# Attention over the memory one head at a time, opening tiles chunk by chunk, and four row gathers issued at four places

## The chip, the cores and the metric

The kernel runs on one core of one Trainium2 chip. The metric is the device time of one execution in microseconds; the time of a kernel is the median of its runs. A profile comes from one execution of its own, whose time may differ a little from that median.

The engines are called as in the profile: PE is TensorE (PEld its weight loads), DVE is VectorE, ACT is ScalarE, POOL is GpSimd, SP is SyncE. Each works through its own queue in order and waits on semaphores.

## The reference

A decoder trunk of two layers on 256 tokens with 1024 channels. Each layer has a token mixer (gated convolution and forgetting attention), a cross-attention over 256 memory tokens, and a SwiGLU channel mixer: dense in layer 0, top 2 of 8 experts in layer 1. The parts that matter here:

```python
def mem_cross_attention(h, m, w_q, w_kv, g_q, g_k):
    q = rmsnorm((h @ w_q).reshape(B, S, XA_HEADS, XA_HEAD_DIM), g_q)      # 4 heads x 128
    kv = (m @ w_kv).reshape(B, M, 2, XA_HEADS, XA_HEAD_DIM)
    k = rmsnorm(kv[:, :, 0], g_k)
    v = kv[:, :, 1]
    s = jnp.einsum('bshd,bmhd->bhsm', q, k) * (XA_HEAD_DIM ** -0.5)
    p = jax.nn.softmax(s, axis=-1)
    return jnp.einsum('bhsm,bmhd->bshd', p, v).reshape(B, S, XA_WIDTH)

for l in range(DEPTH):
    x = x + mixer(rmsnorm(x, g_mix[l])) @ w_out[l]
    x = x + mem_cross_attention(rmsnorm(x, g_xa[l]), rmsnorm(mem, g_mem[l]), ...) @ w_xo[l]
    x = x + (swiglu or moe_swiglu)(rmsnorm(x, g_ffn[l]), ...)
# moe: top-2 of 8 experts per token, softmax of the two logits as weights, sum of the two experts' outputs
```

## The kernel before

**Products.** Every large product is made of three: inputs and weights are split into a high part (ACT, a copy that rounds to fp32r) and a low part (DVE, the value less the high part), and PE adds high x high, low x high and high x low. Weights come in *fills*: SP loads each into one of four slots of `ring`, ACT writes its high part to `wh`, DVE its low part to `wl` (two buffers each, three for the high parts in the expert passes). A slot of `ring` is free when DVE has made the low part; `wh` when PE's high products are done (`highs_used`), `wl` when the low products are. In the queues of ACT and DVE these splits stand at places written out by hand (`high_of`, L765, and `low_of`, L1112).

**PSUM.** Eight banks. `layer_results` lists the results in order, each with the bank it takes (a pair names the result whose bank it inherits, a single name takes the next of `plan.order`). PE waits in `open_bank` until the bank's former result has been read.

**Opening tile.** `channel_tile` (from L1648) makes 128 output channels for 256 tokens from 8 input chunks. Its first call on a new input (`inputs` given) comes while ACT is still writing the chunks' high parts (`input_high`, L795, or L984 for the gate product) and DVE their low parts (`input_low`, L1132): eight products high x high, each pair of chunks behind a wait, then eight with the weights' low part, then eight with the inputs' low part. It is called so for the query projection of each layer (`yT`) and for the first gate tile of layer 0 (`zT`). Each product is 256 wide and shows as L1616.

**Attention over the memory.** The query projection has four tiles, one for each head, two to a bank (`xq0`, `xq1`) and two to a fill. DVE multiplies a pair of heads by the gain (`query_gained`, L1327); ACT squares the pair (L962); PE sums the squares (`query_means`, products with `selh`), DVE adds epsilon (`query_mean`, L1332), and POOL raises to the power -1/2 (L699). PE makes the scores of a head (`memory_scores`, `xk`), DVE their maximum (`memory_max`, L1341, then L1344 with POOL's result), ACT the exponentials (`memory_exps`, L940, two for a head), DVE the normalisation (`probs_normalised`, L1349 and L1350), PE the transposes (`memory_probs`, L1972), DVE or ACT the copy (`probs_copied`, L1354, L949), and PE the sum over the memory (`memory_heads`, `xv`, one bank for two heads), split by ACT (L954) and DVE (L1131). The output projection `xw` runs by slots of two heads each: sixteen high products 512 wide (L1612, L1613), then the second pair of heads (`memory_heads(1)`, put inside), then eight products with the low weights. PE's order is tiles 0 to 2, means of the first pair, tile 3, scores 0 and 1, means of the second pair, scores 2 and 3, transposes 0 and 1, heads 0 and 1, transposes 2 and 3, projection.

**Expert passes.** Layer 1 runs the eight experts one after another, each in a pass of 24 fills: 16 of gate and up weights, 8 of down weights. A token's normalised row stands in the DRAM table `rows_of`, 128 rows to an expert. In every pass POOL stores the results of the expert before to that table (L723) and, after the up product of the first half, loads the next expert's rows (L720); in the last pass no rows are left to load. Instead POOL gathers each token's finished result rows from the table (L734): two choices for each of two token tiles, 128 rows of 4 KB each, four transfers in all. It issues all four as soon as the store of pass seven is done and the last rows have been transposed. DVE adds them to the residual behind the low parts of slots 20 to 23 (`rows_added`, L1519). Slots are counted from 0 here.

```python
            for t in range(TT):
                for c in range(2):
                    nc.gpsimd.indirect_dma_start(rows_got[t][c], None, rows_of, bass.IndirectOffsetOnAxis(ap=rows[:, t, c:c + 1], axis=0)
                                                 ).then_inc(rows_back[2 * t + c], 16)
```

## Time and profile before

| | us |
|---|---|
| median of 3 runs | 1349.35 |
| lowest and highest | 1347.03, 1351.03 |
| the profiled execution's own time | 1347.77 |
| its span, first to last instruction | 1346.2 |
| PE, DVE, ACT, POOL busy | 1316.9, 1019.1, 831.3, 92.0 |
| mean granted TensorE clock | 0.995 |

A span is the time from the first to the last instruction of the profiled execution. Matmuls are pipelined and overlap in the rows: the distance of two starts is what one costs, and the duration is longer. A product of plain fp32 operands shows as two records. The memory attention of layer 0 lies near 155 to 185 us, that of layer 1 near 525 to 555 us; the passes over the experts fill the time from 574 us on, the last from 1241.6 us.

### The profile page before, as it was taken

Reading aid. Unit: us, or ns where it says so; the run is one execution under the profiler, and the core shown is the slowest. Engines: PE = TensorE matmul, PEld = TensorE weight load, DVE = VectorE, ACT = ScalarE, POOL = GpSimd, SP = SyncE. Lnnn points to the kernel's source line nnn. Section 1 sums busy time; section 2 is a strip of 40 time slices with the busy share of each in tenths; the row PEclk is TensorE's granted clock in tenths of the full one; section 3 lists DMA queues with packets and bytes.
Section 4 is the critical chain, followed back from the end, with each engine's and each line's share of the span. In section 5 each row is a group of like instructions: output and inputs, shape, how many; then the busy total and the mean of one; then the engine's idle time right before and its main releaser. Section 6 shows DMA issues by size and latency. Waiting matters only on the chain.

```text
span 1346.2 us, 18754 instructions
## 1 busy us (share of the span) xinstructions
PE 1316.9 (98%) x7213; PEld 1146.7 (85%) x7213; DVE 1019.1 (76%) x782; ACT 831.3 (62%) x738; POOL 92.0 (7%) x98
## 2 busy tenths in 40 slices
PE   7999999999999999899999999999999999999998
PEld 6998879999889988788888888888888888888786
DVE  4758665545366586588888888888889888888888
ACT  5545454343355454477777777678677677777674
POOL 4201010000012010010000000000000000000300
PEclk9999999999999999999999999999999999999999
DMA  8633535554498334289999899899999998998994
GB/s 305 201 119 122 171 136 188 194 182 143 155 316 327 118 122 164 81 326 393 337 414 384 338 409 387 343 412 371 356 388 355 394 380 342 417 385 336 414 386 164
DMA packets 120910, 386.24 MB, mean 287 GB/s; under 512 B 6064, under 2 KB 47644, under 8 KB 120860
## 3 DMA queue, kind: packets, MB, share of 16 engines
q1 hardware_dynamic: 108972, 365.09, 71.8%
q0 software_dynamic: 3168, 11.54, 2.2%
q10 hardware_dynamic: 8720, 8.91, 1.9%
q8 instruction: 36, 0.59, 0.2%
q14 instruction: 14, 0.11, 0.0%
HBM read 369.79 MB, written 15.73 MB: 286 GB/s over the span
## 4 chain that ended last, share of the span: by engine, by line
PE 85%; DVE 7%; ACT 4%; issue 2%; DMA 1%; POOL 1%; SPq 0%; DVEq 0%; ACTq 0%
PE bank L1616 40%; PE bank L1612 21%; PE bank L1613 21%; DVE wl L1112 3%; PE bank L2112 1%; ACT wh L765 1%; DMA ring<-in_we_up 1%; DVE wl L1126 1%; ACT scratch L940 1%; DVE scratch L1259 1%; ACT wh L779 1%; DVE scratch L1237 1%; ACT aT L795 1%; DVE aT_low L1131 1%; PE bank L1792 0%
## 5 line engine op out<-in xcount | busy, mean ns | idle before, releaser
L1126 DVE TENSOR_TENSOR wl<-ring,wh 128x2816 fp32r<-128x2816 f32 (+1 forms) x127 | 400.3, 3171 | 54.6 <-PE bank L1616 42.7
L779 ACT ACTIVATE wh<-ring 128x2816 fp32r<-128x2816 f32 (+1 forms) x128 | 336.6, 2631 | 141.7 <-PE bank L1613 49.1
L1112 DVE TENSOR_TENSOR wl<-ring,wh 128x2048 fp32r<-128x2048 f32 (+2 forms) x69 | 186.6, 2704 | 94.1 <-ACT wh L765 84.3
L1126 DVE TENSOR_TENSOR wl<-ring,wh_third 128x2816 fp32r<-128x2816 f32 (+1 forms) x64 | 187.0, 2923 | 32.4 <-PE bank L1616 28.1
L1612 PE MATMUL bank<-wh,xh 128*128 128x512 f32 x528 | 198.7, 376 | 4.1 <-DVE wl L1126 2.8
L765 ACT ACTIVATE wh<-ring 128x2048 fp32r<-128x2048 f32 (+1 forms) x68 | 152.6, 2244 | 78.8 <-PE bank L1616 38.1
L1613 PE MATMUL bank<-wh,xl 128*128 128x512 f32 x528 | 197.7, 374 | 0.0
L1616 PE MATMUL bank<-wl,xh 128*128 128x512 f32 (+1 forms) x768 | 194.9, 375 | 0.0
L779 ACT ACTIVATE wh_third<-ring 128x2816 fp32r<-128x2816 f32 (+1 forms) x64 | 155.5, 2429 | 35.1 <-DMA ring<-in_we_up 14.8
L1616 PEld LDWEIGHTS bank<-wl,xh 128*128 128x128 f32 x768 | 141.7, 188 | 18.5
L1612 PE MATMUL bank<-wh,ah 128*128 128x512 f32 x328 | 128.7, 393 | 1.7 <-DVE wl L1112 1.7
L1613 PE MATMUL bank<-wh,al 128*128 128x512 f32 x328 | 127.9, 390 | 0.0
L1612 PEld LDWEIGHTS bank<-wh,xh 128*128 128x128 f32 x528 | 99.1, 188 | 23.4 <-issue 4.9
L1613 PEld LDWEIGHTS bank<-wh,xl 128*128 128x128 f32 x528 | 99.2, 188 | 15.2
L1616 PE MATMUL bank<-wl,ah 128*128 128x512 f32 x440 | 112.0, 389 | 0.0
L1612 PE MATMUL bank<-wh,aT 128*128 128x512 f32 (+2 forms) x272 | 98.5, 371 | 0.8 <-DVE scratch L1237 0.5
L1616 PEld LDWEIGHTS bank<-wl,ah 128*128 128x128 f32 x440 | 82.6, 188 | 17.1
L1613 PE MATMUL bank<-wh,aT_low 128*128 128x512 f32 (+2 forms) x272 | 96.9, 365 | 0.0
L1612 PE MATMUL bank<-wh_third,xh 128*128 128x512 f32 (+1 forms) x240 | 90.6, 377 | 0.0
L1613 PE MATMUL bank<-wh_third,xl 128*128 128x512 f32 (+1 forms) x240 | 90.2, 376 | 0.0
L1616 PE MATMUL bank<-xh,wh 128*128 128x256 f32 x352 | 86.4, 284 | 0.8 <-ACT xh L984 0.8
L1616 PE MATMUL bank<-xl,wh 128*128 128x256 f32 x352 | 85.5, 283 | 0.0
(262 smaller groups left out, 1924.4 us busy)
## 6 DMA issues: line engine op xcount, KB each, us to landing
ring<-in_we_gate SPq DMA_DIRECT2D x64, 1408.0 KB, 7.6
ring<-in_we_up SPq DMA_DIRECT2D x64, 1408.0 KB, 7.7
ring<-in_we_down SPq DMA_DIRECT2D x56, 1536.0 KB, 8.4
ring<-in_w_in SPq DMA_DIRECT2D x8, 1536.0 KB, 11.7
ring<-in_w_in SPq DMA_DIRECT2D x10, 1024.0 KB, 6.8
ring<-in_w_gate SPq DMA_DIRECT2D x6, 1536.0 KB, 6.7
ring<-in_w_up SPq DMA_DIRECT2D x6, 1536.0 KB, 6.6
ring<-in_w_down SPq DMA_DIRECT2D x6, 1536.0 KB, 6.6
```

The source lines that it names most:

```text
L765: nc.scalar.activation(wh[:, j, 0:n], ring[:, slot, 0:n], ACT.Copy).then_inc(high_ready, 1)
L779: nc.scalar.activation(wh_in_pass(j, n), ring[:, slot, 0:n], ACT.Copy).then_inc(high_ready, 1)
L795: ins = nc.scalar.activation(aT[:, c, :], bank(l, f"{names}{i}")[:, k * S:k * S + S], ACT.Copy, scale=col(l, gain, c))
L940: ins = nc.scalar.activation(xsc[:, h, q, :], bank(l, f"xs{h}")[:, q * S:q * S + S], ACT.Exp, bias=xnm[:, h, q:q + 1], scale=xqr[:, h, q:q ...
L1112: nc.vector.tensor_tensor(wl[:, j, 0:n], ring[:, slot, 0:n], wh[:, j, 0:n].bitcast(F32), ALU.subtract).then_inc(low_ready, 1)
L1126: nc.vector.tensor_tensor(wl[:, j % 2, 0:n], ring[:, j % NSLOT, 0:n], wh_in_pass(j, n).bitcast(F32), ALU.subtract).then_inc(low_ready, 1)
L1131: return nc.vector.tensor_tensor(dst, src, high_.bitcast(F32), ALU.subtract)
L1237: nc.vector.scalar_tensor_tensor(sc[:, h, :], bank(l, f"s{h}")[:, 0:3 * P], HD ** -0.5, mask[:], ALU.mult, ALU.add).then_inc(take(l, f"s{h ...
L1259: then_wait(nc.vector.scalar_tensor_tensor(acc[:, back:S], u[:, 0:S - back], col(l, "tap", 8 - 4 * back + j), acc[:, back:S], ALU.mult, AL ...
L1612: nc.tensor.matmul(dst, x_high, w_high, start=first, stop=False)
L1613: return nc.tensor.matmul(dst, x_low, w_high, start=False, stop=False)
L1616: return nc.tensor.matmul(dst, lhsT, rhs, start=first, stop=last)
```

## The change

Three things are changed.

1. **Opening tile.** In `channel_tile` with `inputs`, each high x high product is followed at once by the product with the weights' low part of the same chunk. The wait for the low part stands ahead of the tile. The eight products with the inputs' low part come last, as before. The query projection's first tile now has its own bank and signals its end.
2. **Memory attention.** Each head has a bank of its own for its query tile, and gain, square, means, epsilon and power are done for one head at a time: the means go to two spare columns of the head's own bank. The orders of PE, ACT, DVE and POOL are rewritten so that heads follow each other: a tile of the projection, the means and scores of the head before it, the transposes of the head before that. The last head's transposes stand inside the output projection, ahead of the second pair of heads. Banks of later results follow from a new list, `AFTER_MEMORY`, and the scratch region into which ACT writes squares that nobody reads moves from 5120 to 1024.
3. **Gathers.** POOL issues the first gather where it was. Ahead of the second it waits for the up product of the first half to be done (`uA2`, after slot 7), ahead of the third for the transposed hidden block `hA2` (after slot 10), ahead of the fourth for the up product of the second half (`uB2`, after slot 15). Each wait is followed by a one-element addition.

The core of the diff:

```diff
-    names += [f"yT{i}" for i in range(4)] + ["xq0", "xq1"]
-    names += ["xqm0", "xs0", "xs1", "xqm1", "xs2", "xs3", "xpt0", "xpt1", "xo0", "xpt2", "xpt3"]
-    names += [f"xw{i}" for i in range(4)] + ["xo1"] + [f"zT{i}" for i in range(4)]
+    names += ["yT0", "yT1", ("yT2", "wo0"), ("yT3", "wo1"), ("xq0", "wo2"), ("xq1", "wo3"), ("xq2", "oT0"), ("xq3", "oT1")]
+    names += [(f"xqm{h}", f"xq{h}") for h in range(4)] + [(f"xs{h}", f"yT{h}") for h in range(4)]
+    names += [(f"xpt{h}", f"xqm{h}") for h in range(4)] + [("xo0", "xs0")]
+    names += [("xw0", "xpt0"), ("xw1", "xpt1"), ("xw2", "xs1"), ("xw3", "xs2"), ("xo1", "xo0")]
+    names += [("zT0", "xs3"), ("zT1", "xpt2"), ("zT2", "xpt3"), ("zT3", "xo1")]
...
             for t in range(TT):
                 for c in range(2):
+                    if t + c > 0:
+                        pool.wait_ge(*lfull(("uA2", "hA2", "uB2")[2 * t + c - 1], rounds * NE - 1))
+                        then_wait(nc.gpsimd.tensor_tensor(zeros[0:1, 1:2], zeros[0:1, 2:3], zeros[0:1, 3:4], ALU.add))
                     nc.gpsimd.indirect_dma_start(rows_got[t][c], None, rows_of, bass.IndirectOffsetOnAxis(ap=rows[:, t, c:c + 1], axis=0)
                                                  ).then_inc(rows_back[2 * t + c], 16)
...
+                query_square(0)
+                high_of(l, "xo", 0)
+                query_square(1)
+                memory_exps(0)
+                query_square(2)
+                memory_exps(1)
+                query_square(3)
+                probs_copied(1)
+                memory_exps(2)
+                heads_high(0)
+                memory_exps(3)
                 high_of(l, "xo", 1)
-                probs_copied(1)
-                memory_exps(2, 3)
-                heads_high(0)
                 probs_copied(3)
                 heads_high(1)
...
                 if inputs is not None:
                     pe.wait_ge(high_ready, n + 1)
+                    pe.wait_ge(low_ready, n + 1)
                     for k in range(KT):
                         if k % 2 == 0:
                             pe.wait_ge(acthigh_ready, HIGHS[fill[0], inputs] + k // 2 + 1)
                         mm(ps, w_high[:, k, :], x_high[:, k, :], k == 0, False)
-                    pe.wait_ge(low_ready, n + 1)
-                    for k in range(KT):
                         mm(ps, w_low[:, k, :], x_high[:, k, :], False, False)
...
+                query_tile(0)
+                query_tile(1)
+                query_means(0)
                 for i in range(2):
                     pe.wait_ge(*taken(l, f"mkT{i}"))
-                memory_scores(0, 1)
+                memory_scores(0)
+                query_tile(2)
                 query_means(1)
-                memory_scores(2, 3)
-                memory_probs(0, 1)
+                memory_scores(1)
+                memory_probs(0)
+                query_tile(3)
+                query_means(2)
+                memory_scores(2)
+                memory_probs(1)
+                query_means(3)
                 for t in range(TT):
                     pe.wait_ge(*taken(l, f"mv{t}"))
                 memory_heads(0)
-                memory_probs(2, 3)
-                token_projection("xw", "xo", XH, range(2), {j: taken(l, f"xo{j}") for j in range(2)}, lambda: memory_heads(1))
+                memory_scores(3)
+                memory_probs(2)
+
+                def last_heads():
+                    memory_probs(3)
+                    memory_heads(1)
+
+                token_projection("xw", "xo", XH, range(2), {j: taken(l, f"xo{j}") for j in range(2)}, last_heads)
```

DVE's order in the memory attention, from the first gain to the first normalisation. TENSOR_SCALAR to `scratch` is a gain, SCALAR_TENSOR_TENSOR a mean's epsilon, TENSOR_REDUCE a maximum, RECIPROCAL with the TENSOR_TENSOR behind it a normalisation, TENSOR_TENSOR to `wl` the low part of a fill. Before:

```order
L1323 TENSOR_SCALAR msq<-msq 128x2
L1112 TENSOR_TENSOR wl<-ring,wh 128x2048
L1327 TENSOR_SCALAR scratch<-bank,vcols 128x512
L1112 TENSOR_TENSOR wl<-ring,wh 128x2048
L1332 SCALAR_TENSOR_TENSOR xqr<-bank,msq 128x4
L1336 ISA
L1327 TENSOR_SCALAR scratch<-bank,vcols 128x512
L1341 TENSOR_REDUCE xnm<-bank 128x2
L1344 TENSOR_TENSOR xnm<-xnm,xqr 128x2
L1341 TENSOR_REDUCE xnm<-bank 128x2
L1344 TENSOR_TENSOR xnm<-xnm,xqr 128x2
L1349 RECIPROCAL xden<-xden 128x2
```

After the change:

```order
L1336 TENSOR_SCALAR scratch<-bank,vcols 128x256
L1371 TENSOR_SCALAR msq<-msq 128x2
L1124 TENSOR_TENSOR wl<-ring,wh 128x2048
L1336 TENSOR_SCALAR scratch<-bank,vcols 128x256
L1340 SCALAR_TENSOR_TENSOR xqr<-bank,msq 128x2
L1343 ISA
L1348 TENSOR_REDUCE xnm<-bank 128x2
L1351 TENSOR_TENSOR xnm<-xnm,xqr 128x2
L1124 TENSOR_TENSOR wl<-ring,wh 128x2048
L1336 TENSOR_SCALAR scratch<-bank,vcols 128x256
L1356 RECIPROCAL xden<-xden 128x2
```

A gain is for one head now, the first maximum stands ahead of the second fill's low part, and the first normalisation follows that low part and a further gain.

PE's order from the means of the second head to those of the third. The tile products have `aT`, means `selh`, scores `xk`, and transposes `ident`. After the change:

```order
L1632 MATMUL bank<-aT,wl 128x256 x8
L1632 MATMUL bank<-selh,scratch 128x1 x2
L1632 MATMUL bank<-xk,scratch 128x256 x2
L1988 MATMUL bank<-ident,scratch 128x128 x4
L1632 MATMUL bank<-aT,wh 128x256
L1632 MATMUL bank<-aT_low,wh 128x256
```

Before, the same kinds of work, from the last products of the last query tile:

```order
L1616 MATMUL bank<-aT,wl 128x256 x8
L1616 MATMUL bank<-xk,scratch 128x256 x4
L1616 MATMUL bank<-selh,scratch 128x1 x4
L1616 MATMUL bank<-xk,scratch 128x256 x4
L1972 MATMUL bank<-ident,scratch 128x128 x8
L1616 MATMUL bank<-scratch,xv 128x256 x4
```

The first head's transposes now stand ahead of the fourth query tile; before, all tiles and all scores came first.

POOL's order at the end of the program, the gathers and what stands between them, after the change:

```order
L735 TENSOR_TENSOR zeros<-zeros 1x1
L741 DMA memT<-rows_of,rows 128x1024
L739 REGISTER_ALU
L740 TENSOR_TENSOR zeros<-zeros 1x1
L741 DMA row_spare<-rows_of,rows 128x1024
L739 ISA
L740 TENSOR_TENSOR zeros<-zeros 1x1
L741 DMA xk<-rows_of,rows 128x1024
L739 REGISTER_ALU
L740 TENSOR_TENSOR zeros<-zeros 1x1
L741 DMA xv<-rows_of,rows 128x1024
```

Before, the four stood one behind another, behind the first addition. Now each of the last three has a wait and an addition ahead of it.

## Rows read from the trace of the kernel before

**Rows 1.** The page's first part: engine, busy us (share of the span), instructions.
```profile
PE 1316.9 (98%) x7213; PEld 1146.7 (85%) x7213; DVE 1019.1 (76%) x782; ACT 831.3 (62%) x738; POOL 92.0 (7%) x98
```

**Rows 2.** Windows: us, busy (records) per engine, PEclk, DMA share, GB/s; passes seven, eight.
```profile
1147.00:1241.60 94.60, 94.60 (x452) 80.78 (x451) 82.01 (x45) 69.99 (x47) 2.67 (x3) 1.00 0.96 377
1147.00:1181.40 34.40, 34.40 (x164) 29.63 (x163) 30.68 (x13) 26.49 (x15) 2.67 (x3) 1.00 1.02 416
1241.60:1276.00 34.40, 31.60 (x148) 26.71 (x147) 28.78 (x18) 21.96 (x13) 12.71 (x7) 1.00 1.01 413
```

**Rows 3.** Waits of PE, layer 1, 521 to 575 us: total, times, longest.
```profile
PE bank L1972 <- DVE scratch L1350: 1.8, 3, 1.0
```

**Rows 4.** Timeline, layer 1's opening tile: start, us, engine, line, op, tiles, count, idle before.
```profile
522.26 3.03 ACT L795 ACTIVATE aT<-bank,vcols 128x256 fp32r<-128x256 f32 x8 [1.61 <-PE bank L1635]
523.20 3.23 DVE L1132 SCALAR_TENSOR_TENSOR aT_low<-bank,vcols,aT 128x256 fp32r<-128x256 f32 x8 [1.34 <-ACT aT L795]
...
525.68 1.12 PE L1616 MATMUL bank<-aT,wl 128*128 128x256 f32 x8
...
526.64 1.12 PE L1616 MATMUL bank<-aT_low,wh 128*128 128x256 f32 x8
```

**Rows 5.** Timeline, the opening tile of layer 0's gate product, PE.
```profile
195.53 1.11 PE L1616 MATMUL bank<-xh,wl 128*128 128x256 f32 x8
```

**Rows 6.** Timeline, the same stretch, PE: means, transposes, last heads, low products.
```profile
538.85 1.02 PE L1616 MATMUL bank<-selh,scratch 128*128 128x1 f32 x8
...
539.74 1.97 PE L1616 MATMUL bank<-xk,scratch 128*128 128x256 f32 x8
...
547.13 0.63 PE L1972 MATMUL bank<-ident,scratch 128*128 128x128 f32 x4 [0.47 <-DVE scratch L1350]
...
551.41 1.89 PE L1616 MATMUL bank<-scratch,xv 128*128 128x256 f32 x8
552.94 2.18 PE L1616 MATMUL bank<-wl,aT 128*128 128x512 f32 x8
554.96 0.39 PE L1612 MATMUL bank<-wh,aT 128*128 128x512 f32 x1
```

**Rows 7.** Timeline, layer 1's memory attention on the engines beside PE.
```profile
528.36 2.29 DVE L1112 TENSOR_TENSOR wl<-ring,wh 128x2048 fp32r<-128x2048 f32 x1
...
530.68 0.75 DVE L1327 TENSOR_SCALAR scratch<-bank,vcols 128x512 f32<-128x512 f32 x1
...
536.46 1.01 POOL L699 TENSOR_TENSOR xqr<-xqr,neghalf 128x4 f32<-128x4 f32 x1 [30.85 <-DVEq L1336]
...
538.19 0.69 DVE L1341 TENSOR_REDUCE xnm<-bank 128x2 f32<-128x512 f32 x1
...
539.12 0.56 ACT L940 ACTIVATE scratch<-bank,xnm,xqr 128x256 f32<-128x256 f32 x1 [0.34 <-DVE xnm L1344]
...
540.55 0.69 DVE L1350 TENSOR_TENSOR scratch<-scratch,xden 128x512 f32<-128x512 f32 x1
```

**Rows 8.** Timeline of POOL, last pass: the first and the last of four gathers.
```profile
1249.91 1.06 POOL L734 DMA_INDIRECT memT<-rows_of,rows  x1 [0.28 <-POOL zeros L731]
...
1258.31 3.86 POOL L734 DMA_INDIRECT xv<-rows_of,rows  x1 [0.30 <-issue]
```

**Rows 9.** Chain of waits: the same low products of passes seven and eight.
```profile
1180.25 1.29 PE bank L1616 x6
...
1278.13 1.28 PE bank L1616 x6
```

**Rows 10.** Timelines: slot 6 in pass seven (ACT), in pass eight (ACT, PE).
```profile
1162.72 2.56 ACT L779 ACTIVATE wh<-ring 128x2816 fp32r<-128x2816 f32 x1 [0.89 <-DMA ring<-in_we_gate]
...
1261.11 2.56 ACT L779 ACTIVATE wh<-ring 128x2816 fp32r<-128x2816 f32 x1 [3.51 <-DMA ring<-in_we_gate]
...
1267.03 0.47 PE L1612 MATMUL bank<-wh,xh 128*128 128x512 f32 x1 [2.37 <-DVE wl L1126]
```

**Rows 11.** Timeline of DVE, last pass: the low part of slot 6.
```profile
1263.79 3.09 DVE L1126 TENSOR_TENSOR wl<-ring,wh 128x2816 fp32r<-128x2816 f32 x1 [1.57 <-ACT wh L779]
```

More of the change, by code:

```diff
@@ L135, in build @@
                 plan.add((l, n))
+        plan.order, plan.turn = [plan.at[l, m][0] for m in AFTER_MEMORY], 0
         if l == 0:
@@ L955, in heads_high, with query_square @@
                                          bank(l, f"xo{i}")[:], ACT.Copy).then_inc(yhigh_ready, 1)
[L957 to L964 removed]
+                def query_square(h):
+                    act.wait_ge(*full(l, f"xq{h}"))
+                    act.wait_ge(xq_gained, XH * l + h + 1)
+                    nc.scalar.activation(sq[:, 4 + h, :], bank(l, f"xq{h}")[:, 0:S], ACT.Square).then_inc(take(l, f"xq{h}"), 1)
+                query_square(0)
[9 more added lines that the diff above has]
+                memory_exps(3)
                 high_of(l, "xo", 1)
[L966 to L968 removed]
                 probs_copied(3)
```

96 lines of the change are left out of this document (45 added, 51 removed).

## The prediction

> **What bounds the kernel now.** The page comes first: PE holds records for 98% of the span [rows 1], so only what shortens PE's work or its gaps can move the end. The windows show where gaps are. A middle pass over an expert has PE busy for 94.60 of 94.60 us at a granted clock of 1.00, with DMA at 0.96; in its first 34.4 us DMA is at 1.02, full. The last pass has 31.60 busy us in the same 34.4, so 2.8 us of gap [rows 2]. The other gaps lie in the attention over the memory, once per layer: 1.8 us in three waits of the transposes for DVE's normalised probabilities [rows 3]. Ahead of it the opening tile of the query projection is paced: ACT writes the eight input chunks in 3.03 us, DVE their low parts in 3.23 us, and PE does the eight products with the weights' low parts only when the last chunk is there [rows 4]. Three places, then: openings, attention, gathers.
>
> **Openings.** The eight low-weight products start at 525.68 and the next eight at 526.64: 0.12 us each [rows 4]. Six of them now run while ACT makes the chunks (one pair of chunks per about 0.75 us, four products take 0.48). The last pair of highs is there at 525.3, so PE is through with them at 525.8; six products with the low inputs follow to 526.5, and the last low chunk is there at 523.20 + 3.23 = 526.43, just in time. The tile ends 0.7 earlier. The new wait for the weights' low part ahead of the tile costs nothing: DVE made it before the residual. The same helper opens layer 0's gate product, where the pattern is the same [rows 5]: 0.7 too. What is late next there is PE itself.
>
> **Memory attention, per layer.** PE's work stays: 0.96 us for eight tile products, 0.9 for a pair of means (538.85, then 539.74), about 0.8 for a head's scores, 0.55 for a head's transposes, 1.53 for a pair of heads (551.41 to 552.94), 0.23 for each product 512 wide [rows 6]. What moves is who waits. I lay the new order out on layer 1's clock with these durations: DVE's weight low part 2.29, a gain 128x512 0.75 (taken as 0.42 for half), a max 0.69, a normalisation 0.69 and 0.2 of reciprocal, an exponential 0.56 twice for a head, a power on POOL 1.01 (for half the elements 0.75 to 1.01) [rows 7], 0.05 to 0.3 for each hop.
> PE: tile 0 ends 526.8, tile 1 529.7, means 0 and scores 0 530.9, tile 2 533.8, means 1 and scores 1 535.0. DVE: its weight low part keeps it until 530.65 [rows 7], then gain 1, mean 0, max 0 (behind POOL's power) to 532.5, the next weight low part to 534.85, gain 2, normalisation 0 at 536.2. So PE waits 1.2 us ahead of transposes 0. Then tile 3 to 539.7, means 2, scores 2 540.9; DVE, held by the wait for tile 3, ends normalisation 1 at 541.15: 0.3 of wait. Transposes 1, means 3, heads 0 to 543.7, scores 3 to 544.5; normalisation 2 ends 544.65: 0.2. The projection's sixteen high products start at 545.4 behind DVE's low part of the heads and hide head 3's maximum, exponentials and normalisation (ready 548.3). Head 3's transposes and the second pair of heads end at 551.3, the eight low products at 553.1; ACT's and DVE's copies of the second pair take as long, so the next slot starts near 553.2. Before, it started at 554.96 [rows 6]: 1.8 saved, opening included. A check from the other side: 29.7 us passed since the last chunk, and PE's work in them is 26.6 (90 tile products 10.8, means 1.7, scores 3.3, transposes 2.2, heads 3.1, 24 wide products 5.5), so 3.1 was waiting; now 27.9 with 25.9 of work leave 2.0.
> In layer 0 everything stands as in layer 1, 370 us earlier; behind it ACT and DVE split the first gate slot in the order of their queues, ahead of the residual sum. Both start from the second pair of heads, so this too comes 1.8 earlier. Added instructions: per layer two gains, two means, two squares, two powers; they are in the layout. The bank changes and the moved scratch region cost nothing, since each bank taken has been read 5 us or more before.
> Weighed against a rule: by the row, a gain of 128x512 takes 0.75, and a chunk of 128x256 in the same form 3.23/8 = 0.40 [rows 4, 7], so halving adds 0.05 per pair, and the sum stays. The Trainium skill (VectorE: DVE Perf Modes, "The TRN2 errata") says that each small operation pays a fixed latency and advises at least 512 elements; with its 150 cycles (0.16 us, an estimate from that page) four extra DVE operations per layer would cost 0.6 each layer if all were on the path, and the sum would be 5.3 instead of 6.5.
>
> **Gathers.** Four transfers of 0.52 MB start between 1249.91 and 1258.31 [rows 8], 5.1 us of DMA at 413 GB/s, in the stretch where DMA is full [rows 2]. By the chain the same products come at 1180.25 and 1278.13; a pass is 94.60, so the last pass loses 3.3 us [rows 2, 9]. Slot 6 (the seventh of 24) is converted 19.5 us after the pass began, in the pass before 15.7 [rows 2, 10]. The change leaves the first gather there (1.27 us), puts the second where every other pass loads 0.52 MB of rows, and the others after a hidden block and after the last up product. Of 5.1 us of extra transfer 1.8 were swallowed, so 1.27 alone would be. But DVE has one-off work in this pass (the last pass's weights), which also makes it late: slot 6's low part would, without the wait of 1.57 for ACT, start near 1262.4 and end 1265.5 [rows 11]; PE is free at 1267.03 - 2.37 = 1264.66 [rows 10], and starts that slot only with the low part. So about 1 us of loss stays and 2.2 go. Bounds: 1.3 (two gathers' worth still felt) and 3.3 (nothing lost). The later gathers are cheap if the later slots' slack holds; they are first needed by DVE after slots 21 to 23, 15 us or more after issue, and POOL has nothing behind its new waits.
>
> **Sum.** 2 x 1.8 + 0.7 + 2.2 = 6.5 us off the profiled execution's 1347.77: 1341.3. The median of the three runs is 1.58 above that execution, so 1342.8. A measurement tells about 0.3%, 4 us: faster means under 1345.3.
>
> **Rivals.** (a) The gathers' load only moves. The bytes are the same, DMA is at 0.96 in a whole pass [rows 2], so a late gather can starve a down slot as an early one starved slot 6; against it, the last pass fetches nothing for a next one. Gain 0 there: 4.3 saved, 1345.0. The Trainium skill (DMA: Bandwidth & Descriptors, "Issuing engines are not separate DMA queues") says that transfers of every issuing engine run on the same 16 DMA engines and interleave; the trace agrees so far that slot 6 was late beside POOL's gathers.
> (b) The round trip scores, maximum, power, exponentials, normalisation is longer than the tile, means and scores that cover it. It is 535.0 to 536.2 late already at head 0. If each of three heads waits 0.8 more, 4.8 goes back: 1347.6, no change.
> (c) The same mechanism on the other side: DVE is in order, and gain 3 and the weight low part stand ahead of a normalisation that PE waits for. At 1.1 us more at each of six rounds the saving is gone, above 1.8 it is slower; with 2.3, as long as one weight low part [rows 7], it is 13.8 - 6.5 = 7.3 slower: 1356.6. For it: one chain of four heads on one DVE, busy for most of that time. Against: the page of before shows two rounds with waits of at most 1.0 [rows 3].
> (d) All waits vanish: 1.9 more per layer and 1.1 in the pass, 11.4 saved, 1337.9.
>
> **How the numbers follow.** Forecast 0.60, own range 1340.5 to 1344.5; (a) 0.15; (b) 0.12; (c) 0.06; (d) 0.07. Of (a), at the edge of what can be told, 0.10 counts as faster and 0.05 as same. Faster 0.60 + 0.07 + 0.10 = 0.77, same 0.12 + 0.05 = 0.17, slower 0.06. The range takes in (a), half of (d) and the run-to-run spread of 2 us: 1339.5 to 1346.5.
>
> **What would show it.** In the profile after: in layer 1 the opening tile's low-input products end about 0.7 earlier against the last chunk; three waits of transposes near 1.2, 0.3 and 0.2; the second projection slot 27.9 us after the last input chunk (now 29.7). In the last pass slot 6 starts with a wait near 1, not 2.37, four gathers stand apart, and PE has no new gap after slot 8. Wrong would be waits of PE over 2 us at a head, a PE gap beside the third or fourth gather, or a granted clock below 1.00 in the attention.

## The result, and the profile after

| | before | after |
|---|---|---|
| median of 5 runs, us | 1349.68 | 1341.64 |
| lowest and highest | 1347.03, 1351.03 | 1339.31, 1342.32 |
| the profiled execution's own time | 1347.77 | 1339.31 |
| its span | 1346.2 | 1337.7 |

The ratio is 0.9942, 95% interval 0.9929 to 0.9956: faster by 8.0 us, with 5.9 to 9.6 inside the interval. The prediction said 1342.8 and a gain of 6.5. Beside the experiments below the kernel before ran 9 to 29 times each, with medians of 1347.8 to 1348.1, so the 1349.68 here lies high: against those medians the changed kernel is 6.1 to 6.5 us faster, and the stretches below give 7.5.

The page's first part after the change. PE is still at 98%, with 1.9 us less of records [rows 1]:

```profile
PE 1315.0 (98%) x7213; PEld 1145.5 (86%) x7213; DVE 1020.1 (76%) x790; ACT 831.8 (62%) x742; POOL 84.2 (6%) x105
```

**Where the time went.** In both profiles I took the starts of the same six events and subtracted. PE's transposes of the token mixer near 51 us stand for the start; then come the first input chunk of layer 1's query projection, DVE's `hT` (the router's input), ACT's table load behind the router, the first low products on the hidden block in pass seven, and the last such group of six in the last pass. The rows of after:

```profile
51.08 1.04 PE L1769 MATMUL bank<-ident,scratch 128*128 128x128 f32 x8
...
519.68 3.03 ACT L802 ACTIVATE aT<-bank,vcols 128x256 fp32r<-128x256 f32 x8 [1.62 <-PE bank L1651]
...
557.05 1.29 DVE L1149 TENSOR_TENSOR hT<-bank,vcols 128x512 f32<-128x512 f32 x2 [0.41 <-PE bank L1651]
...
557.89 3.71 PE L1632 MATMUL bank<-wr,hT 128*128 128x8 f32 x32 [0.22 <-DVE hT L1149]
...
563.99 1.28 ACT L1031 ACT_TABLE_LOAD   x1
...
1205.95 1.52 PE L1632 MATMUL bank<-wl,ah 128*128 128x512 f32 x6
...
1327.52 1.52 PE L1632 MATMUL bank<-wl,ah 128*128 128x512 f32 x6
```

Before (its first chunk is in [rows 4]):

```profile
50.78 1.04 PE L1752 MATMUL bank<-ident,scratch 128*128 128x128 f32 x8
...
561.72 1.29 DVE L1137 TENSOR_TENSOR hT<-bank,vcols 128x512 f32<-128x512 f32 x2 [0.40 <-PE bank L1635]
...
563.11 4.61 PE L1616 MATMUL bank<-wr,hT 128*128 128x8 f32 x32 [0.77 <-DVE hT L1137]
...
570.11 1.28 ACT L1019 ACT_TABLE_LOAD   x1
...
1212.16 1.53 PE L1616 MATMUL bank<-wl,ah 128*128 128x512 f32 x6
...
1336.03 1.52 PE L1616 MATMUL bank<-wl,ah 128*128 128x512 f32 x6
```

| stretch | before | after | gain | forecast |
|---|---|---|---|---|
| start to layer 1's first chunk (all of layer 0) | 471.48 | 468.60 | 2.88 | 1.8 + 0.7 |
| first chunk to `hT` (layer 1's attention) | 39.46 | 37.37 | 2.09 | 1.8 |
| `hT` to table load (router) | 8.39 | 6.94 | 1.45 | 0 |
| table load to pass seven | 642.05 | 641.96 | 0.09 | 0 |
| pass seven to the end of the last pass | 123.87 | 121.57 | 2.30 | 2.2 |

They sum to 8.81, less 0.30 of a later start: the 8.5 us between the spans. The router's 1.45 us was in no term of mine.

**Layer 1's attention.** Of PE's waits between 518 and 575 us in after, those up to the router's first product:

```profile
PE bank L1988 <- DVE scratch L1357: 0.5, 2, 0.4
PE bank L1632 <- ACT aT L802: 0.4, 1, 0.4
PE bank L1632 <- DVE hT L1149: 0.2, 1, 0.2
```

The transposes now wait 0.5 us in all, 1.8 before [rows 3]. The timeline of the same stretch:

```profile
523.35 1.12 PE L1632 MATMUL bank<-aT_low,wh 128*128 128x256 f32 x8
...
524.50 0.48 DVE L1336 TENSOR_SCALAR scratch<-bank,vcols 128x256 f32<-128x256 f32 x1 [0.65 <-PE bank L1632]
...
528.67 0.70 POOL L703 TENSOR_TENSOR xqr<-xqr,neghalf 128x2 f32<-128x2 f32 x1 [25.69 <-DVEq L1343]
...
532.37 0.69 DVE L1357 TENSOR_TENSOR scratch<-scratch,xden 128x512 f32<-128x512 f32 x1
...
533.21 0.63 PE L1988 MATMUL bank<-ident,scratch 128*128 128x128 f32 x4 [0.37 <-DVE scratch L1357]
...
538.17 0.63 PE L1988 MATMUL bank<-ident,scratch 128*128 128x128 f32 x4 [0.15 <-DVE scratch L1357]
...
550.28 0.39 PE L1628 MATMUL bank<-wh,aT 128*128 128x512 f32 x1
```

The low-input products of the opening tile start 3.67 us after the first chunk, 4.38 before [rows 4]: 0.71 won. The second projection slot starts at 550.28, 27.57 us after the last chunk (519.68 + 3.03).

**The last pass.** Windows, as in [rows 2], of pass seven, of its first 34.4 us, and of the last pass's:

```profile
1140.72:1235.32 94.60, 94.60 (x452) 80.78 (x451) 82.01 (x45) 69.71 (x48) 1.95 (x3) 1.00 0.96 377
1138.90:1173.30 34.40, 34.40 (x163) 29.59 (x162) 30.07 (x13) 26.78 (x15) 1.95 (x3) 1.00 1.02 417
1233.50:1267.90 34.40, 33.57 (x158) 28.65 (x157) 31.19 (x21) 24.93 (x15) 5.57 (x6) 1.00 1.02 415
```

PE's gap in the last pass is 0.8 us where it was 2.8. Slot 6 on ACT, DVE and PE, then the gathers on POOL:

```profile
1253.15 2.56 ACT L786 ACTIVATE wh<-ring 128x2816 fp32r<-128x2816 f32 x1 [1.70 <-DMA ring<-in_we_gate]
...
1256.02 3.09 DVE L1138 TENSOR_TENSOR wl<-ring,wh 128x2816 fp32r<-128x2816 f32 x1 [0.21 <-DVE ffn L1518]
...
1259.26 0.47 PE L1628 MATMUL bank<-wh,xh 128*128 128x512 f32 x1 [0.83 <-DVE wl L1138]
```

```profile
1243.78 3.91 POOL L741 DMA_INDIRECT memT<-rows_of,rows  x1 [0.36 <-POOL zeros L735]
...
1267.63 0.97 POOL L741 DMA_INDIRECT row_spare<-rows_of,rows  x1 [0.27 <-POOL zeros L740]
...
1280.33 0.96 POOL L741 DMA_INDIRECT xk<-rows_of,rows  x1 [0.27 <-POOL zeros L740]
...
1299.49 0.96 POOL L741 DMA_INDIRECT xv<-rows_of,rows  x1 [0.27 <-POOL zeros L740]
```

ACT's wait for the gate weights fell from 3.51 to 1.70 us [rows 10] in this pair of profiles, and DVE no longer waits for ACT ahead of slot 6 (1.57 before [rows 11]). It comes straight from a one-off operation of the last pass (L1518).

### The profile page after: what moved, and what is told of

The parts are those of the page before. It is cut to its first block, busy times and chain, and to the rows that moved or that the text cites. A ratio compares the mean times of both kernels' runs of the same rounds, so it can differ in the third digit from the quotient of the medians.

```text
span 1337.7 us, 18771 instructions
## 1 busy us (share of the span) xinstructions
PE 1315.0 (98%) x7213; PEld 1145.5 (86%) x7213; DVE 1020.1 (76%) x790; ACT 831.8 (62%) x742; POOL 84.2 (6%) x105
## 4 chain that ended last, share of the span: by engine, by line
PE 87%; DVE 8%; ACT 2%; issue 1%; DMA 1%; POOL 1%; SPq 0%; DVEq 0%; ACTq 0%
PE bank L1632 40%; PE bank L1628 22%; PE bank L1629 22%; DVE wl L1124 3%; PE bank L2140 1%; DVE wl L1138 1%; ACT wh L772 1%; DMA ring<-in_we_gate 1%; DVE scratch L1271 1%; DVE scratch L1249 1%; DVE aT_low L1143 1%; PE bank L1809 0%; POOL mfox L672 0%; ACT wh L786 0%; PE bank L1651 0%
## 5 line engine op out<-in xcount | busy, mean ns | idle before, releaser
L1124 DVE TENSOR_TENSOR wl<-ring,wh 128x2048 fp32r<-128x2048 f32 (+2 forms) x69 | 186.6, 2705 | 94.5 <-ACT wh L772 84.6
L1632 PEld LDWEIGHTS bank<-wl,ah 128*128 128x128 f32 x440 | 82.6, 188 | 17.1
```

Source lines behind the costliest of these rows:

```text
L1124: nc.vector.tensor_tensor(wl[:, j, 0:n], ring[:, slot, 0:n], wh[:, j, 0:n].bitcast(F32), ALU.subtract).then_inc(low_ready, 1)
L1632: return nc.tensor.matmul(dst, lhsT, rhs, start=first, stop=last)
```

## The experiments

Theory: the three parts act on their own (openings 0.7 each, head-by-head order about 1.4 per layer, gathers 2.2 to 2.7), and a fourth effect, the bank of the router's result, explains what I had missed. Twelve kernels were run; every one has a profile, so the same stretches can be compared. "Half clock" is the time between 558 and 580 us in which PEclk was 0.50 (1.2 of 2.4 GHz), added up from windows of 0.5 us. The other columns are differences of starts as above, in us.

| kernel | median | ratio to before, interval | start to chunk | chunk to `hT` | `hT` to table | `hT` to pass 7 | pass 7 to end | half clock |
|---|---|---|---|---|---|---|---|---|
| before | | | 471.48 | 39.46 | 8.39 | 650.44 | 123.87 | 10.2 |
| b_gathers_alone | 1346.32 | 0.9985 (0.9976, 0.9994) | 471.47 | 39.50 | 8.22 | 650.15 | 121.54 | 10.2 |
| b_opening_alone | 1346.66 | 0.9989 (0.9980, 0.9999) | 470.01 | 38.77 | 9.57 | 651.63 | 123.27 | 13.7 |
| b_router_bank | 1347.33 | 0.9996 (0.9987, 1.0004) | 471.52 | 39.47 | 7.32 | 649.46 | 123.64 | 10.2 |
| a_attention_alone | 1346.30 | 0.9981 (0.9970, 0.9992) | 473.10 | 39.48 | 6.94 | 649.11 | 122.64 | 6.8 |
| a_opening_undone | 1344.95 | 0.9971 (0.9960, 0.9982) | 469.94 | 38.04 | 7.06 | 651.69 | 121.67 | 10.2 |
| a_gathers_together | 1343.25 | 0.9967 (0.9956, 0.9978) | 468.59 | 37.35 | 6.94 | 648.90 | 124.24 | 6.8 |
| a_router_bank | 1343.40 | 0.9961 (0.9948, 0.9974) | 468.61 | 37.40 | 9.22 | 652.23 | 121.50 | 13.7 |
| after | 1341.64 | 0.9942 (0.9929, 0.9956) | 468.60 | 37.37 | 6.94 | 648.90 | 121.57 | 6.8 |
| c_oneoffs_later | 1343.13 | 0.9965 (0.9952, 0.9979) | 468.62 | 37.38 | 6.94 | 649.69 | 122.40 | 6.8 |
| c_first_gather_later | 1342.86 | 0.9961 (0.9948, 0.9975) | 468.65 | 37.34 | 8.43 | 652.22 | 122.66 | 13.7 |
| c_gathers_all_late | 1342.65 | 0.9961 (0.9948, 0.9975) | 470.22 | 37.38 | 7.06 | 649.45 | 122.49 | 10.2 |
| c_both_later | 1342.19 | 0.9958 (0.9944, 0.9971) | 468.67 | 37.34 | 8.19 | 650.28 | 121.65 | 10.2 |
| d_spread | 1340.93 | 0.9940 (0.9928, 0.9952) | 468.60 | 37.41 | 8.28 | 651.08 | 120.59 | 13.7 |

Where nothing was changed the first two stretches and the last repeat within 0.1 us, but for places named below; the medians scatter by more than most single edits are worth. The stretches therefore carry the argument, and the medians say only whether it holds in sum. By the ratios the three parts alone give 2.0 (gathers), 1.5 (openings) and 2.6 us (attention), 6.1 together, and the whole change 7.8; the intervals reach 1.2 to 1.9 us to either side, so the two agree, but weakly.

Two entries under `hT` to pass 7 hold a loss that belongs to no edit. Between the same products of neighbouring passes 94.6 to 94.7 us lie everywhere else, but 96.87 once in a_opening_undone and 95.75 once in c_first_gather_later. In the first ACT waited for weights in the middle of a pass that has no gathers:

```profile
872.48 2.56 ACT L786 ACTIVATE wh<-ring 128x2816 fp32r<-128x2816 f32 x1 [4.40 <-DMA ring<-in_we_gate]
```

The four weight transfers issued from 862.3 on took 10.0 to 11.4 us to land there, those in the same place of after 6.9 to 8.5. Why is open.

**Opening tiles: undone in after, and alone in before.**

The edit against after; b_opening_alone has its reverse, in the kernel before.

```diff
-                    pe.wait_ge(low_ready, n + 1)
                     for k in range(KT):
...
                         mm(ps, w_high[:, k, :], x_high[:, k, :], k == 0, False)
+                    pe.wait_ge(low_ready, n + 1)
+                    for k in range(KT):
                         mm(ps, w_low[:, k, :], x_high[:, k, :], False, False)
```

> The changed kernel with the opening tile's products in their old order (eight high, then eight with the weights' low part). My theory: each of three openings (query projection of both layers, gate product of layer 0) is 0.7 us longer and nothing hides it, 2.1 us slower than the change in all, about 1343.7. Rival (the head-by-head order hides the late tile, since DVE's chain sets the pace there): only layer 0's gate product counts, 0.7 us; the PE wait ahead of the first transposes falls from 0.4 to 0.

> The kernel before, with each high product of an opening tile followed by the low-weight product of its chunk and nothing else. My theory: three openings of 0.65 to 0.7 us each, 2.0 us in all: 0.65 in layer 0's attention, 0.65 at layer 0's gate tile, 0.65 in layer 1; time 1345.8. Rival: the tile's gain is taken back by the next wait (PE comes earlier to a product that DVE's low part of the second fill holds, or to the transposes): then the transposes' waits grow from 1.8 to 2.4 and 0.7 us or less is left of each attention.

Chunk to `hT` is 0.67 longer without the new order and 0.69 shorter with it alone. The whole of layer 0 (start to chunk), which has two openings, is 1.34 longer and 1.47 shorter. So 0.67 to 0.74 for an opening, three times, and nothing is given back. The rival of b_opening_alone, a growing wait at the transposes, fell: they wait 1.8 us there as before. So did that of a_opening_undone, a late tile hidden by DVE's chain: PE still waits ahead of the first transposes, 0.28 where after has 0.37. The median of b_opening_alone is only 1.3 us below before; the difference to 2.1 is within what its runs scatter (1343.5 to 1350.2). That of a_opening_undone is 3.3 above after, not 2.1; in its profile, besides the 2.0 of the openings, 2.3 us are the loss in a middle pass named above.

```profile
535.95 0.63 PE L1989 MATMUL bank<-ident,scratch 128*128 128x128 f32 x4 [0.28 <-DVE scratch L1357]
```

**Attention head by head alone** (after with both other parts undone).

> The changed kernel with both other parts undone: gathers all at once, old order in the opening tiles; what is left is the attention head by head (with its bank plan). The three parts add up if they are independent: the whole is 8.0 us, gathers 2.5, openings 2.0, so this one is 3.5 us faster than before: 1.2 to 1.4 in each layer's attention and 0.5 to 1.4 around the router. Time 1344.3 where before is 1347.8. Rival: the attention has most of its gain only with the new opening, because the round trips through DVE start from it; then under 2 us is left.

By the stretches of a_opening_undone, which has the same attention and old openings, the head-by-head order is worth 39.46 - 38.04 = 1.42 in layer 1, and 471.48 - 469.94 = 1.54 in layer 0. With 0.7 for the opening this gives 2.1 to 2.2 per layer. No run takes the order of the heads, their banks and the moved scratch region apart; the 1.4 to 1.5 is for all of these together. But a_attention_alone itself shows 39.48 in layer 1, nothing won, and its median is 1.6 us below before, not 3.5: taken alone, that is what the rival forecast. The windows say why:

```profile
523.50:527.50 4.00, 3.02 (x19) 2.19 (x18) 2.82 (x8) 3.77 (x9) 0.00 (x0) 1.00 0.36 149
527.50:531.00 3.50, 3.50 (x19) 3.50 (x18) 0.97 (x5) 2.12 (x4) 0.00 (x0) 0.52 0.03 5
```

The same two stretches of the program in a_opening_undone, by distance from the first chunk:

```profile
521.55:525.55 4.00, 3.02 (x19) 2.19 (x18) 2.83 (x8) 3.77 (x9) 0.00 (x0) 1.00 0.35 148
525.55:529.05 3.50, 3.50 (x32) 3.50 (x31) 2.10 (x5) 2.48 (x4) 0.00 (x0) 1.00 0.02 5
```

In one the granted clock is 0.52 and 19 products have records, in the other 1.00 and 32. The program is the same here, and so is PE's work in the 4 us ahead (3.02 us busy in both), so this is a matter of the execution, not of the order. It cost 39.48 - 38.04 = 1.44 us. The windows show two more such stretches in that profile, at 155.0 to 159.5 (0.62) and 350 to 360 (0.83); after has none between its start event at 51 us and the router. Start to chunk is 3.2 us longer than in a_opening_undone, which has the same program up to there and neither stretch. Without the three, the stretches would add up as the theory says. Its twelve runs lie between 1343.0 and 1349.1, but such stretches do not explain this: the run of 1349.14 had a mean granted clock of 0.994, one of 1347.93 had 0.996, and the three with 0.992, the profiled one among them, 1346.1 to 1347.9. What scatters the runs of one kernel is open.

**Gathers: together again in after, and at four places in before.** The edit takes out or puts in the waits for `uA2`, `hA2`, `uB2` and their additions.

> The changed kernel with its four gathers issued at one place again. My theory (the early gathers starve slot 6 of the last pass): the last pass loses 3.3 us again instead of about 1, so this is 2.3 us slower than the change, about 1344; slot 6 of the last pass starts with a wait near 2.4 us. Rival (the gathers' load only moves, and the shorter last pass came from something else): no difference to the change, 1341.6, and the wait stays near 0.8.

> The kernel before, with the gathers issued at the four places and nothing else. My theory: 2.3 to 2.7 us less in the last pass (97.9 us between the same low products of passes seven and eight becomes 95.3 to 95.6), PE's waits there 0.8 instead of 2.8; time 1345.3 on a scale where before is 1347.8. Rival: what the gathers give depends on the shorter attention ahead of them; then less than 1.5.

Pass seven to the end grows by 2.67 in one and shrinks by 2.33 in the other. The size is as expected, the place is not: a_gathers_together has no wait of 2.4 us at slot 6, but 1.17 there, 1.05 at slot 7 and 0.78 further on. Its PE waits for low parts in the last pass, and ACT's rows for slots 6 and 7:

```profile
PE bank L1625 <- DVE wl L1135: 3.0, 3, 1.2
```

```profile
1252.56 2.57 ACT L783 ACTIVATE wh<-ring 128x2816 fp32r<-128x2816 f32 x1 [1.54 <-DMA ring<-in_we_gate]
...
1258.43 2.55 ACT L783 ACTIVATE wh<-ring 128x2816 fp32r<-128x2816 f32 x1 [3.31 <-DMA ring<-in_we_up]
```

So the 3.51 of slot 6 in before [rows 10] is one way in which the same delay falls. In the other four profiles with four gathers at the start slot 6 waits 1.2 to 1.5 us and slots 7 and 8 2.8 to 3.3 each. The sum of ACT's waits ahead of slots 6, 7 and 8 is steady: 7.4 to 7.8 us with four gathers (five profiles), 4.0 with one (five; in a_opening_undone one of the three waits is put down to PE), 2.7 with none (four).

That the gathers' worth depends on what stands ahead is not seen: 2.33 and 2.67 differ by less than the executions do. It is not the same in every execution, though: five profiles with the four gathers in a bunch at the start have 122.64 to 124.24 (mean 123.53), four with the change's places 121.50 to 121.67 (mean 121.57). On average 1.96 us, in one execution 1.1 to 2.7.

**The router's bank.** After the change the plan puts the router's result `r` into a bank that has long been read. Before, `r` came after `zT2` in its bank, and the first product had to wait for DVE's copy of `zT2`, one of the four pieces of `hT`. Two kernels turn this round:

```diff
-            for n, b in (("r", 4), ("rank0", 5), ("rank1", 6)):
+            for n, b in (("r", 5), ("rank0", 4), ("rank1", 6)):
```

> The changed kernel with the router's result put in the bank that holds the third transposed tile of the layer's output (rank0 takes the bank freed), as it stood by chance in the kernel before. My theory: the router's first product waits for that tile to be copied, and the stretch from there to the first expert pass is 1.4 us longer: 0.5 us of wait and 0.9 us because the granted clock falls to 0.50 before the router's products are over, not after. Total about 1343. Rival (bank and clock have nothing to do with each other): 0.5 us, clock at 1.00 through the router's products. Second rival (the 1.4 us come from elsewhere): no difference.

> The kernel before, with the router's result in a bank that none of the transposed tiles uses (rank0 takes the other one). My theory: 1.4 us faster than the kernel before, 1348.2, with the router's 32 records in 3.7 instead of 4.6 us at clock 1.00. Rival (only the wait goes): 0.5 us. Rival (elsewhere): none.

The first router product of a_router_bank, then of b_router_bank:

```profile
559.36 5.44 PE L1632 MATMUL bank<-wr,hT 128*128 128x8 f32 x32 [0.77 <-DVE hT L1149]
```

```profile
562.67 4.09 PE L1616 MATMUL bank<-wr,hT 128*128 128x8 f32 x32 [0.22 <-DVE hT L1137]
```

The wait is 0.77 with the old relation and 0.22 with the new, both ways: 0.55 us by the bank plan. My theory said more, 1.4 us from bank and clock together. It fell: from `hT` b_router_bank reaches pass seven 0.98 us sooner than before (its median is 0.6 us lower, with no change inside the interval), and a_router_bank 3.33 us later than after. The rest of the stretch goes with the clock. The 32 products take 3.71 us where PEclk stays at 1.00, and 5.44 where it falls to 0.50 at 561.0, inside them. When it falls differs from one profile to the next (560.4 to 568.6 us), and so does how long it stays there: 6.8, 10.2 or 13.7 us. What this costs is read from `hT` to the first low products on the hidden block in the first pass, ahead of the two losses named above. With the new relation that took 81.3 to 82.1 us in the four profiles with 6.8, 81.8 to 82.6 in the four with 10.2 and 83.4 and 83.5 in the two with 13.7; with the old one 82.5 and 82.8 with 10.2, 84.0 and 84.6 with 13.7. Before has 82.81 and after 81.27; less the 0.55 of the bank, 1.0 us of this goes with the clock, and I count it as luck of the two executions. That is not settled: none of the four profiles with the old relation had 6.8, and four of the ten with the new one had. What decides the fall is open.

**The 1 us that is left in the last pass.** The prediction put it down to DVE's one-off operations. Four kernels tested this. c_oneoffs_later moves them behind slots 12 to 15; c_first_gather_later issues no gather at the start; c_both_later does both; c_gathers_all_late has all four behind `uB2`.

> The changed kernel, with DVE's one-off operations of the last pass (the counts, the weights of the last choices, the two one-hot blocks) moved from behind the low parts of slots 2 to 6 to behind those of slots 12 to 16. My theory: the 1.0 us that the last pass still loses, and the one wait of PE for DVE's low part (0.8 us), come from these operations, about 2.9 us of DVE work ahead of slot 6's low part. Then the wait is gone, and the last pass takes 0.8 to 1.0 us less against the pass before (94.7 instead of 95.6 us between the same low products), the time about 1340.8. Rival: the wait comes from the first gather, whose transfer still makes the gate weights late; then the wait stays at 0.6 to 0.8 and the time at 1341.6. Second rival: DVE has as little slack later; a new wait of PE appears in slots 13 to 18 and the 1.0 us comes back there.

> The changed kernel, with the first gather also issued behind the up product of the first half, so that two gathers stand there one behind the other and none at the start of the pass. My theory (DVE's one-off operations make slot 6 late): the wait of 0.8 us for DVE's low part stays at 0.6 to 0.8 although the weights of slots 5 and 6 now come earlier, and the last pass still loses 0.8 to 1.0 us; time 1341.6. Rival (the first gather's transfer is the cause): the wait is gone and the pass loses under 0.3; time 1340.8. Two gathers beside each other after slot 7 may give a new wait of up to 0.6 us in slots 8 to 11.

> The two edits together: one-off operations of DVE behind the low parts of slots 12 to 16, and the first gather behind the up product of the first half beside the second. If the one-offs are the cause of the remaining loss, this is as fast as that edit alone, about 1340.7; if each holds half of it, it is the only one of the three with no wait of PE in the last pass, 0.4 us below either. If the later slots have no slack, a wait of PE of 0.5 to 1.0 us appears after slot 12 and the time stays at 1341.6.

> The changed kernel, with all four gathers issued in one bunch behind the up product of the second half, after slot 15. Theory one: what costs at the start of the pass is that DMA is full there; later in the last pass nothing is fetched for a following pass, so the bunch costs nothing and the last pass loses 1.0 us or less (time 1341.6 or 0.3 less). Rival: what costs is the bunch itself, about 5 us of transfers at once, wherever it stands; then PE waits about 2.7 us more at slots 18 to 21, or at the end of the program DVE's adding of rows waits for the gathers, and the time is 1343.5 to 1345.

Two things must be put right. The moved one-offs stand behind slots 12 to 15, not 12 to 16 as the expectations say: `last_gates` is the last of them, behind slot 15. And my condition for c_first_gather_later and c_both_later put a wait ahead of the first gather and took out those of the second and third, so three gathers, not two, stand behind `uA2` (POOL rows at 1271.62, 1272.98 and 1276.18 in the first). The start of the pass, which they were made for, is as stated. PE's waits for low parts in the last pass, by kernel; c_oneoffs_later:

```profile
1263.57 0.47 PE L1626 MATMUL bank<-wh,xh 128*128 128x512 f32 x1 [0.31 <-DVE wl L1138]
...
1292.52 0.47 PE L1626 MATMUL bank<-wh_third,xh 128*128 128x512 f32 x1 [0.71 <-DVE wl L1138]
```

c_first_gather_later:

```profile
1263.21 0.47 PE L1628 MATMUL bank<-wh,xh 128*128 128x512 f32 x1 [0.82 <-DVE wl L1138]
...
1296.09 0.47 PE L1628 MATMUL bank<-wh_third,xh 128*128 128x512 f32 x1 [0.81 <-DVE wl L1138]
```

c_both_later:

```profile
1293.30 0.47 PE L1626 MATMUL bank<-wh_third,xh 128*128 128x512 f32 x1 [0.72 <-DVE wl L1138]
```

c_gathers_all_late, which has a second one near 1330 (0.42):

```profile
1261.14 0.46 PE L1628 MATMUL bank<-wh,xh 128*128 128x512 f32 x1 [0.62 <-DVE wl L1138]
```

So neither theory holds alone. Measured to the first group of six low products behind slots 6 and 7 and against d_spread (below), which has no wait there, the one-offs without a gather cost 1.04 us (0.84 in c_gathers_all_late, which has them without a gather too), the first gather without the one-offs 0.77, both together 0.98, and neither nothing. Each is enough, and removing one of them wins 0.2 us or less. My rows for the prediction were right, and its reading, one cause, was too narrow. What was moved also came back further on: the one-offs in a bunch behind slots 12 to 15 cost 1.0 us there, three gathers behind `uA2` likewise, both together (c_both_later) again no more than that, and four behind `uB2` 1.05 us at the last two slots (ACT and, behind it, DVE's low parts wait for late down weights, ACT once 3.47 us). The theory of c_gathers_all_late had this bunch cost nothing, its rival 2.7 us; neither holds. A bunch of gathers cost something in all three places, least at the end.

**Both causes taken out and spread.** DVE's waits in the rows of c_both_later say where a one-off fits: 1.57 us ahead of slot 4's low part, 1.59 ahead of that for `hA2`; and those of after show 0.57 to 0.76 ahead of slots 14 to 16.

```diff
-                    if t + c > 0:
-                        pool.wait_ge(*lfull(("uA2", "hA2", "uB2")[2 * t + c - 1], rounds * NE - 1))
+                    if 2 * t + c < 3:
+                        pool.wait_ge(*lfull(("uA2", "hA2", "uB2")[2 * t + c], rounds * NE - 1))
...
+                lows(2, 3)
                 if last:
                     last_rows()
...
                     last_weights()
...
+                lows(*range(4, 9))
...
+                if last:
+                    last_choice(0, gated, 0, 1)
                 hidden_low("A", 2)
-                lows(*range(12, 17))
+                lows(12, 13)
+                if last:
+                    last_choice(1, oneh, 0)
+                lows(14)
+                if last:
+                    last_choice(1, oneh, 1)
+                lows(15)
+                if last:
+                    last_gates()
+                lows(16)
```

> The changed kernel, with the gathers behind the first half's up product, behind hA2, and two behind the second half's up product (none at the start of the pass), and with DVE's one-off operations laid where the rows of the former kernels show DVE idle: the counts and weights behind the low part of slot 3 (1.57 us idle there before slot 4's low part in the kernel with both moved), the first one-hot block ahead of hA2's low part (1.59 idle), the second in halves behind slots 13 and 14 and the gates behind slot 15 (0.57 to 0.76 idle each). My theory: two causes hold the last pass back, the DMA load of the first gather and the one-offs ahead of slot 6, and each alone is enough for 0.3 to 0.8 us; with both gone and neither bunched elsewhere PE has no wait for a low part in the last pass, the distance from the first group of six low-weight products on the hidden block in pass seven to the last of the last pass is 120.7 instead of 121.57 us, and the time 0.8 to 0.9 below the changed kernel's (about 1340.9 where before is 1347.9). Rival: a later stage has its own limit (DVE in slots 13 to 18), and what is won at slot 6 is lost there: the distance stays at 121.4 to 121.7 and the wait of 0.7 us appears after slot 13.

```profile
1208.88 1.53 PE L1632 MATMUL bank<-wl,ah 128*128 128x512 f32 x6
...
1329.47 1.52 PE L1632 MATMUL bank<-wl,ah 128*128 128x512 f32 x6
```

The distance is 120.59, 0.98 less than in after, as expected (120.7), and between the same products of passes seven and eight 94.62: the last pass loses nothing any more. No wait for a low part is left in it, and the rival, a new wait after slot 13, fell. PE's only wait there is for `memT`, 0.5 us at the end, which after has too:

```profile
PE bank L1632 <- ACT memT L1081: 0.5, 1, 0.5
```

Median 1340.93 (1338.85 to 1341.23), ratio 0.9940 (0.9928 to 0.9952). By the medians this can't be told from after's 0.9942, since a microsecond is below what they resolve. By the last pass of the profile it is the best of the kernels; its span (1339.7) is 2.0 us above that of after, with a half-clock stretch of 13.7 us against 6.8.

## Why the prediction was right

- **Openings, 0.7 each.** Right, in size and reason: 0.71 in layer 1 by the rows, 0.67 to 0.74 by two kernels and three places.
- **Attention, 1.8 per layer.** Measured 2.09 and 2.11 (in layer 0 from the first chunk to the gate's input, 40.07 to 37.96, from the ACT rows at 192.13 and 190.25). The waits ahead of the transposes were forecast at 1.2, 0.3 and 0.2 and came as 0.37, 0.15 and none: 1.2 us less of waiting, but only 0.3 more of gain. By difference, PE's own work and hops were about 0.9 us longer than laid out; no run takes this apart. The layout's first number shows the kind of error: PE came to transposes 0 at 535.4 on the old clock instead of 535.0, and DVE's normalisation ended at 535.6 instead of 536.2. Two errors of half a microsecond met in one wait.
- **The weighed rule.** A gain of half the size takes 0.48, two of them 0.21 more than one of 0.75 [rows 7]; POOL's power 0.70 for two columns, against 1.01 for four. The Trainium skill (VectorE: DVE Perf Modes, "The TRN2 errata") states such a fixed cost of about 150 cycles for operations that read SBUF, 0.16 us as an estimate from that page; the gains here read a PSUM bank and show 0.21 for each added one. Either way it did not decide: the added operations lie beside PE's work, and the attention came out 0.3 better than my sum, not 0.6 worse.
- **Gathers, 2.2.** Measured 2.30 in this pair of profiles, 1.96 on average, within the bounds of 1.3 to 3.3. The statement that 1 us remains was right (0.98), its cause half right: DVE's one-offs do make slot 6 late, but the first gather alone costs 0.77 of it, where the prediction let one gather be swallowed whole ("so 1.27 alone would be"). The place was also read from one execution: in the other four with a bunch at the start slot 6 did not stand out.
- **Rival (a), the load only moves,** fell for the four places. It holds in part for a bunch: four late ones lose 1.05 of what they gain at the start. The page named with it (the Trainium skill, DMA: Bandwidth & Descriptors, "Issuing engines are not separate DMA queues") says that the transfers interleave, and the traces agree: ACT's waits ahead of slots 6 to 8 sum to 7.4 to 7.8 us with four gathers ahead of them, 4.0 with one and 2.7 with none. With none, ACT's wait for the gate weights of slot 6 is 0.91, about the 0.89 of pass seven [rows 10]; in c_first_gather_later:

```profile
1256.31 2.56 ACT L786 ACTIVATE wh<-ring 128x2816 fp32r<-128x2816 f32 x1 [0.91 <-DMA ring<-in_we_gate]
```

- **Rivals (b) and (c), a round trip that becomes the bound,** fell: no wait at a head is over 0.37.
- **The step that failed:** "The bank changes and the moved scratch region cost nothing, since each bank taken has been read 5 us or more before." In the attention itself no wait of PE for a bank is seen. But a new plan moves what comes behind as well, and one wait of 0.55 us at the router went away. With it and the larger terms of the attention the change's own gain is 2.88 + 2.09 + 0.55 + 1.96 = 7.5 us; 6.5 had been forecast, and about 1 us of the profiles' 8.5 goes with the clock at the router. The median lies 1.2 us below the forecast of 1342.8; the five runs scatter by 3.0.

## What to carry to other kernels

When a bank or buffer plan is rewritten, list the waits of every later result in a changed bank, not only of those in the rewritten part. Where one instruction is late for two reasons, taking one away shows next to nothing (0.2 us of 1.0 here); find both in the rows of the engine that is late (a one-off ahead of it, a transfer that feeds it) and take them out together, into places where that engine is seen idle. And where edits are worth one microsecond in 1340, compare distances between the same events of two profiles rather than medians, after reading the granted clock of both.

## What the runs showed of the hardware that I had not expected

- The granted clock falls to 0.50 around the router in every profile, but at different points of the same program and for 6.8 to 13.7 us; from `hT` to the first pass's products the profiles with the longest stretch took 1.9 us more than those with the shortest (means with the new bank relation). Before the fall PE had gone from full work to the router's narrow products (128x8) or was idle behind them; after the fall 32 of these took up to 5.8 us instead of 3.7 (b_opening_alone). Eight of the 14 profiles have one more such stretch between 12 and 17 us, ahead of the start event, and six have none there.
- The same fall can come elsewhere, and then slow dense work: in a_attention_alone PEclk was 0.52 for 3.5 us in which PE had records all the time. In the 4 us ahead, the opening tile with its waits of 0.2 to 0.4 us, PE had been busy for 3.02, and eight products 256 wide took 1.29 us (starts 527.16 and 528.45) instead of 0.96. This cost 1.44 us. Four other profiles with the same opening order (before, b_gathers_alone, b_router_bank, a_opening_undone) ran through it at 1.00. The fall near 353 us in a_attention_alone came behind a wait of 1.75 us; after has the same wait (1.74 at 350.41) and no fall. c_gathers_all_late has one such stretch too, from 351.6 us on, and its way from start to chunk is 1.6 us longer.
- The same last pass with the same four gathers in a bunch took 122.64 us in one profile (a_attention_alone) and 124.24 in another (a_gathers_together), 1.1 and 2.7 more than with the gathers apart. PE's waits for low parts were two in one and three in the other; why is open. One profile would have told either story.
- A pass without gathers can lose time to late weights too: 2.3 us in one middle pass of a_opening_undone, behind transfers that took 10.0 to 11.4 us to land.
